# Gate arithmetic of a ConvFFN up-projection moved from SBUF scratch into PSUM banks, and a layer loop written out

## The chip, the cores and the metric

One core of one Trainium2 chip runs the program. The metric is device time in microseconds (us) of one execution. TensorE (PE) does the matmuls, VectorE (DVE) and ScalarE (ACT) the elementwise work, GpSimd (POOL) one subtraction per weight unit, and SyncE (SP) issues the weight loads.

## The reference

Two decoder layers run over 256 prompt tokens and 8 x 8 sample tokens, T = 320 columns in all. The part that the change touches is the second half of each layer, the ConvFFN:

```
h2 = rms_norm(x, p['norm2_g'])
a, b = jnp.split(h2 @ p['w_up'], 2, axis=-1)              # each (tokens, 2816)
a_seq = jnp.concatenate([conv_buf, a], axis=1)            # two earlier rows in front
c = p['conv_b'] + sum(a_seq[:, j:j + L] * conv_w[j] for j in range(3))
x = x + (jax.nn.gelu(c) * b) @ p['w_down']
new_buf = a_seq[:, a_seq.shape[1] - 2:]
```

## The kernel before

Weights come as units of 128 x 1024 floats, 148 per layer, in the order of use. Every matmul is made of three, so that it is nearly exact in float32: a unit is split into a rounded part `whi` and a rest `wlo`, activations into `hh`/`hl` or `oh`/`ol`, and the products whi x hi, whi x lo and wlo x hi add up in one PSUM bank. SP loads unit n into slot n % 4 of `raw` when that slot's last unit is split (L222). ACT makes `whi` (`hi`, L267), POOL makes `wlo` (`lo`, L231) into one of two slots, once PE is done with the unit two before. A unit is 24 matmuls of 128 x 128 by 128 x 320. All order between engines comes from counting semaphores; each engine works its program off in the order in which it is written.

The feature dimension of the ConvFFN is 22 tiles of 128 rows (FT). They are worked in two groups, 12 (FA) and 10 (FB): the up-projection of the group (`ups`), then its down-projection (`downs`). One tile is a pair of units: unit a into one PSUM bank, unit b into the next. Two pairs are in flight in four banks (A and C for the first group, B for the second); `s` is the pair's parity. Per layer that makes 24 + 12 + 20 + 10 = 66 units from the first up-unit to the last down-unit.

What follows for a pair, by line. DVE: L896 and L897 multiply bank a by the inverse rms `rs` into `apad` in SBUF, behind the two earlier rows that ACT puts there (L542). L901, L902 and L904 are the three taps of the convolution, SBUF to SBUF through three scratch tiles `cc`. ACT: L547 and L548 copy the convolution's new state out, L550 is the gelu into `gg`. DVE: L907 multiplies bank b by `rs` into `tb`, L909 and L910 multiply `gg` by `tb` into `ff`. ACT: L554 rounds `ff` into `oh`. DVE: L913 subtracts to get `ol`. ACT's two splits `hi(u + 4)` and `hi(u + 5)` of later units stand between these steps, the second behind the gelu. PE starts pair j when `ff` of pair j - 2 is there:

```
pe.wait_ge(f_ready, lv * FT + i * 2 + (j0 + s - 1 + 8))
up_unit(u0 + 2 * s, i, banks[2 * s], first)
up_unit(u0 + 2 * s + 1, i, banks[2 * s + 1])
```

The two layers are a hardware loop on each engine (`Fori`, L296 on ACT, L647 on DVE, L1022 on PE), and so are the pairs within `ups`; waits then take their values from registers. At the layer's end DVE adds the down-projection to `x` (L922), then at the next layer's start makes `hl` of the memory tokens (L652) and sums squares (L614), which PE reads in a matmul with ones (L1012).

Of the kernel before, what the change touches and what calls it, by code (L numbers as in the profile page):

```python
# [26 lines left out]
T = SEQ + NS  # L27
# [20 lines left out]
def build_trunk(nc, w, x_in, mem_in, cache_k, cache_v, st_in, consts, final_g,  # L48
# [6 lines left out]
    with ctx:  # L55
# [132 lines left out]
        ap_ready = sem("a_scaled")  # L188
        a_ready, c_ready, g_ready, f_ready, fh_ready, fl_ready = (sem(n) for n in ("conv_state_in_place", "conv_ready", "gelu_ready", "ff_ready", "ff_hi", "ff_lo"))
# [5 lines left out]
        carrier = sem("wait_carrier")  # L195
# [8 lines left out]
        def _(sp):  # L204
# [12 lines left out]
            with sp.Fori(1, DEPTH * UNITS // 4) as i:  # L217
                for s in range(4):
                    src = w[sp.snap(i * 4 + s)]
                    sp.wait_ge(hi_ready, i * 4 + s - 3)  # L220
                    sp.wait_ge(lo_ready, i * 4 + s - 3)
                    sp.dma_start(raw[:, s, :], src).then_inc(loaded[s], 16)  # L222


        @block.gpsimd
        def _(pool):
            def lo(u, s, l, iv=0):

                pool.wait_ge(hi_ready, l * UNITS + iv + u + 1)
                pool.wait_ge(unit_done, l * UNITS + iv + u - 1)  # L230
                pool.tensor_tensor(out=wlo[:, s % 2, :], in0=raw[:, s, :], in1=whi[:, s, :].bitcast(f32),  # L231
                                   op=ALU.subtract).then_inc(lo_ready, 1)

            with pool.Fori(0, DEPTH) as l:
# [3 lines left out]
                pool.wait_ge(hi_ready, l * UNITS + 2)  # L238
                pool.tensor_tensor(out=wlo[:, 1, :], in0=raw[:, 1, :], in1=whi[:, 1, :].bitcast(f32),
                                   op=ALU.subtract).then_inc(lo_ready, 1)  # L240
                lo(2, 2, l)
                lo(3, 3, l)
                with pool.Fori(1, UNITS // 4) as i:
                    for s in range(4):
                        lo(s, s, l, i * 4)
                pool.wait_ge(lo_ready, (l + 1) * UNITS)
# [3 lines left out]
        def _(act):  # L250
# [45 lines left out]
            with act.Fori(0, DEPTH) as lv:  # L296
                l[0] = lv
# [237 lines left out]
                def ups(u0, n, j0):  # L535
                    with act.Fori(0, n // 2) as i:
                        for s in range(2):
                            u = u0 + 2 * s
                            k = i * 2 + (s + j0)
                            sv = apad[s][:, 258:338].rearrange("p (b t) -> p b t", b=8)  # L540
                            act.wait_ge(f_ready, lv * FT + i * 2 + (j0 + s - 1 + 8))
                            nc.scalar.activation(sv[:, :, 0:2], par[:, bass.ds(k * 16 + C_CS, 16)].rearrange("p (b t) -> p b t", b=8),  # L542
                                                 ACT.Copy).then_inc(a_ready, 1)
                            done(u, i * 4)
                            hi(u + 4, i * 4)
# [5 lines left out]
                            done(u + 1, i * 4)  # L551
                            hi(u + 5, i * 4)
                            act.wait_ge(f_ready, lv * FT + i * 2 + (j0 + s + 1) + 8)
                            nc.scalar.activation(oh[:, i * 2 + s, :], ff[:, s, :], ACT.Copy).then_inc(fh_ready, 1)  # L554

                ups(U_UP1, FA, 0)
# [3 lines left out]
                ups(U_UP2, FB, FA)  # L560
                act.wait_ge(fh_ready, lv * FT + FT)
# [28 lines left out]
        def _(dve):  # L590
# [40 lines left out]
            dve.sem_inc(f_ready, 8)  # L631
# [15 lines left out]
            with dve.Fori(0, DEPTH) as lv:  # L647
                l[0] = lv
# [134 lines left out]
                for p in range(4):  # L783
# [25 lines left out]
                    dve.sem_inc(carrier, 1)  # L809
# [72 lines left out]
                def ups(j0, n, banks, u0):  # L882
                    base = dve_n[0]
                    dve.sem_inc(carrier, 1)
                    with dve.Fori(0, n // 2) as i:
                        def lk(ins, k):
# [56 lines left out]
        def _(pe):  # L943
# [78 lines left out]
            with pe.Fori(0, DEPTH) as lv:  # L1022
# [259 lines left out]
                def ups(u0, n, j0, banks, peel):  # L1282
# [6 lines left out]
                    with pe.Fori(1 if peel else 0, n // 2) as i:  # L1289
                        for s in range(2):  # L1290
                            up_pair(u0, j0, s, i, banks)
# [149 lines left out]
```

## Time and profile before

| | us |
|---|---|
| median of 3 runs | 1429.87 (1428.28 to 1432.77) |
| span of the profiled execution, first to last instruction | 1425.8 |
| median less that span | 4.07 |
| PE busy | 1301.5 (91%) |
| DVE busy | 837.2 (59%) |
| ACT busy | 582.5 (41%) |
| POOL busy | 714.2 (50%) |

Times below are from the start of that span. Matmuls are pipelined and their ends are modelled, so a matmul row's own duration (0.31 us) is longer than the distance to the next (0.15 us); the distance is what counts. Idle time of an engine costs something only where another waits for it.

### The profile page before, as it was taken

How to read it: one execution, taken by the hardware profiler on the slowest of the kernel's cores; microseconds unless marked ns; L12 is line 12 of the kernel's file. 1: busy time of each engine (PE TensorE's matmuls, PEld its weight loads, DVE VectorE, ACT ScalarE, POOL GpSimd, SP SyncE). 2: the span in 40 equal slices, each digit the busy share in tenths (PEclk: the TensorE clock that was granted, in tenths of full speed). 3: DMA queues.
4: the chain of work that ended last, by engine and by line, in shares of the span. 5: the costliest groups of instructions: out<-in, count | busy, mean ns of one | idle time of the engine just before them, and what ended most of it. 6: DMA issues, size and time to landing. Idle time of an engine off the chain costs nothing.

```text
span 1425.8 us, 24778 instructions
## 1 busy us (share of the span) xinstructions
PE 1301.5 (91%) x8240; PEld 1233.4 (87%) x8240; DVE 837.2 (59%) x1247; ACT 582.5 (41%) x951; POOL 714.2 (50%) x298
## 2 busy tenths in 40 slices
PE   3999998999999889988978999899999988899886
PEld 3799887999999879988968988899999988898885
DVE  4543328654776775378453541546749587726874
ACT  5472224433444544333444532324443545533342
POOL 2653324444666556655655343434446655566553
PEclk9999999999999999999989999999999999999998
DMA  7435333332444333433554444324334433344342
GB/s 288 148 120 191 133 106 128 117 115 91 149 147 135 116 117 128 152 120 117 178 176 142 148 148 144 111 90 135 124 115 148 141 126 104 117 148 148 103 145 74
DMA packets 53364, 191.90 MB, mean 135 GB/s; under 512 B 6048, under 2 KB 7328, under 8 KB 52896
## 3 DMA queue, kind: packets, MB, share of 16 engines
q1 hardware_dynamic: 43632, 159.15, 32.8%
q10 hardware_dynamic: 9648, 31.60, 6.2%
q8 instruction: 56, 0.92, 0.3%
q14 instruction: 28, 0.23, 0.0%
HBM read 182.20 MB, written 8.53 MB: 134 GB/s over the span
## 4 chain that ended last, share of the span: by engine, by line
PE 62%; DVE 21%; issue 7%; ACT 5%; POOL 2%; DMA 1%; DVEq 1%; ACTq 1%; SPq 0%; POOLq 0%
PE bank L989 27%; PE bank L958 18%; PE bank L1002 6%; DVE ol L913 5%; DVE arena L901 3%; DVE arena L902 3%; DVE arena L904 3%; ACT whi L267 2%; PE bank L1183 2%; POOL wlo L231 2%; DMA raw<-w 1%; PE bank L1086 1%; PE bank L1073 1%; DVE arena L896 1%; ACT oh L554 1%
## 5 line engine op out<-in xcount | busy, mean ns | idle before, releaser
L231 POOL TENSOR_TENSOR wlo<-raw,whi 128x1024 fp32r<-128x1024 f32 x292 | 709.3, 2430 | 668.7 <-PE bank L989 338.6
L267 ACT ACTIVATE whi<-raw 128x1024 fp32r<-128x1024 f32 x294 | 308.1, 1051 | 216.7 <-PE bank L958 91.3
L958 PE MATMUL bank<-hh,whi 128*128 128x320 f32 x832 | 266.7, 321 | 50.6 <-ACT whi L267 50.2
L989 PE MATMUL bank<-oh,whi 128*128 128x320 f32 x848 | 286.3, 338 | 19.6 <-DVE arena L754 8.9
L989 PE MATMUL bank<-ol,whi 128*128 128x320 f32 x848 | 283.5, 334 | 0.0
L989 PE MATMUL bank<-oh,wlo 128*128 128x320 f32 x848 | 282.8, 333 | 0.0
L958 PE MATMUL bank<-hl,whi 128*128 128x320 f32 x832 | 263.9, 317 | 0.0
L958 PE MATMUL bank<-hh,wlo 128*128 128x320 f32 x832 | 263.6, 317 | 0.0
L958 PEld LDWEIGHTS bank<-hh,whi 128*128 128x128 f32 x832 | 162.2, 195 | 58.6 <-ACT whi L267 56.9
L989 PEld LDWEIGHTS bank<-oh,whi 128*128 128x128 f32 x848 | 167.1, 197 | 27.4 <-issue 15.5
L989 PEld LDWEIGHTS bank<-oh,wlo 128*128 128x128 f32 x848 | 167.1, 197 | 3.4 <-issue 1.1
L989 PEld LDWEIGHTS bank<-ol,whi 128*128 128x128 f32 x848 | 167.2, 197 | 3.1 <-issue 0.2
L958 PEld LDWEIGHTS bank<-hh,wlo 128*128 128x128 f32 x832 | 162.3, 195 | 0.0
L958 PEld LDWEIGHTS bank<-hl,whi 128*128 128x128 f32 x832 | 162.0, 195 | 0.2
L958 PE MATMUL bank<-oh,whi 128*128 128x320 f32 x416 | 129.1, 310 | 7.3 <-POOL wlo L231 7.3
L958 PE MATMUL bank<-oh,wlo 128*128 128x320 f32 x416 | 128.5, 309 | 0.0
L958 PE MATMUL bank<-ol,whi 128*128 128x320 f32 x416 | 128.5, 309 | 0.0
L913 DVE TENSOR_TENSOR ol<-arena,oh 128x320 f32 x44 | 98.7, 2244 | 34.0 <-ACT oh L554 34.0
L477 ACT ACTIVATE arena<-bank,par 128x320 f32<-128x320 f32 x48 | 25.3, 528 | 150.1 <-PE bank L989 150.1
L958 PEld LDWEIGHTS bank<-oh,whi 128*128 128x128 f32 x416 | 78.1, 188 | 9.2 <-issue 6.9
L958 PEld LDWEIGHTS bank<-ol,whi 128*128 128x128 f32 x416 | 78.1, 188 | 0.0
L958 PEld LDWEIGHTS bank<-oh,wlo 128*128 128x128 f32 x416 | 78.1, 188 | 0.0
(192 smaller groups left out, 1875.3 us busy)
## 6 DMA issues: line engine op xcount, KB each, us to landing
raw<-w SPq DMA_DIRECT2D x296, 512.0 KB, 3.3
arena<-cache_k ACTq DMA_DIRECT2D x16, 512.0 KB, 5.2
arena<-cache_v ACTq DMA_DIRECT2D x16, 512.0 KB, 4.3
arena<-st_in ACTq DMA_DIRECT2D x8, 512.0 KB, 5.0
sst_out<-arena ACTq DMA_DIRECT2D x8, 512.0 KB, 2.7
arena<-mem_in ACTq DMA_DIRECT2D x2, 1024.0 KB, 6.2
con<-consts SPq DMA_DIRECT2D x1, 1288.0 KB, 13.1
x<-x_in SPq DMA_DIRECT2D x2, 640.0 KB, 9.2
```

Source lines behind the costliest of these rows:

```text
L231: pool.tensor_tensor(out=wlo[:, s % 2, :], in0=raw[:, s, :], in1=whi[:, s, :].bitcast(f32), op=ALU.subtract).then_inc(lo_ready, 1)
L267: nc.scalar.activation(whi[:, s, :], raw[:, s, :], ACT.Copy).then_inc(hi_ready, 1)
L477: nc.scalar.activation(G[:, j, :], A[u % 2][:, 0:T], ACT.Sigmoid, bias=par[:, C_BG + j:C_BG + j + 1]).then_inc(evac, 1)
L554: nc.scalar.activation(oh[:, i * 2 + s, :], ff[:, s, :], ACT.Copy).then_inc(fh_ready, 1)
L901: lk(V.tensor_scalar(cc[s][0][:, 0:336], apad[s][:, 0:336], cw(0), par[:, bass.ds(jw + C_CB, 1)], ALU.mult, ALU.add), 5 * s + 2)
L902: lk(V.scalar_tensor_tensor(out=cc[s][1][:, 0:336], in0=apad[s][:, 1:337], scalar=cw(1), in1=cc[s][0][:, 0:336], op0=ALU.mult, op1=ALU.add ...
L904: V.scalar_tensor_tensor(out=cc[s][2][:, 0:336], in0=apad[s][:, 2:338], scalar=cw(2), in1=cc[s][1][:, 0:336], op0=ALU.mult, op1=ALU.add).t ...
L913: V.tensor_tensor(out=ol[:, i * 2 + s, :], in0=ff[:, s, :], in1=oh[:, i * 2 + s, :].bitcast(f32), op=ALU.subtract).then_inc(fl_ready, 1)
L958: r = MM(out, a, b, start=first and i == 0, stop=last and i == 2, skip_group_check=True)
L989: r = MM(o, a, b[:, k, 0:n], start=k == 0 and i == 0, stop=k == KT_ - 1 and i == 2, skip_group_check=True)
L1002: r = MM(banks[a][:, :], x_[:, k, t0:t0 + P], w_, start=k == 0 and j == 0, stop=k == KT_ - 1 and j == 2, skip_group_check=True)
L1183: r = MM(B[2 + j // 2][:, (j % 2 * 2 + e) * P:(j % 2 * 2 + e + 1) * P], kTm[64:128, e, j * P:(j + 1) * P], vt[64:128, p // 2, 2, h * P:(h ...
```

## The change

The scratch tiles `cc`, `tb` and `ff` are dropped. ACT starts the convolution: it applies the first tap and the bias to `apad` and writes the result into bank a, whose matmul output has been read by then. DVE adds the other two taps in place in that bank. The gelu reads the bank. Bank b is multiplied by `rs` in place, then by `gg` in place, and both `oh` and `ol` are made from it. So each of the Vector instructions of a pair has one operand in PSUM. PE may start pair j only when `ol` of pair j - 2 is written (`fl_ready`), since the banks hold the data until then. The two state copies on ACT become one of 18 columns. All hardware loops, the layers' too, are written out, so waits take constants and no engine jumps back.

```diff
# ACT, per pair
-                            act.wait_ge(ap_ready, lv * FT + i * 2 + (j0 + s + 1))
-                            nc.scalar.activation(cout[:, k, 0:2], apad[s][:, 256:258], ACT.Copy)
-                            nc.scalar.activation(cout[:, k, 2:18].rearrange("p (b t) -> p b t", b=8), sv[:, :, 8:10], ACT.Copy)
-                            act.wait_ge(c_ready, lv * FT + i * 2 + (j0 + s + 1))
-                            nc.scalar.activation(gg[s][:, 0:336], cc[s][2][:, 0:336], ACT.Gelu_apprx_tanh).then_inc(g_ready, 1)
+                        act.wait_ge(ap_ready, 2 * (lv * FT + j + 1))
+                        act.wait_ge(a_ready, lv * FT + j + 1)
+                        nc.scalar.activation(ac[:, 0:336], apad[s][:, 0:336], ACT.Identity, scale=par[:, C_CW + j:C_CW + j + 1],
+                                             bias=par[:, C_CB + j:C_CB + j + 1]).then_inc(c0_ready, 1)
+
+                        nc.scalar.activation(cout[:, j, :].rearrange("p (b t) -> p b t", b=9),
+                                             apad[s][:, 248:338].rearrange("p (b t) -> p b t", b=9)[:, :, 8:10], ACT.Copy).then_inc(cv_ready, 1)
+                        act.wait_ge(c_ready, lv * FT + j + 1)
+                        nc.scalar.activation(gg[s][:, 0:336], ac[:, 0:336], ACT.Gelu_apprx_tanh).then_inc(g_ready, 1)
...
-                            nc.scalar.activation(oh[:, i * 2 + s, :], ff[:, s, :], ACT.Copy).then_inc(fh_ready, 1)
+                        nc.scalar.activation(oh[:, t, :], bc[:, 0:T], ACT.Copy).then_inc(fh_ready, 1)
# DVE, per pair
-                            lk(V.tensor_scalar(cc[s][0][:, 0:336], apad[s][:, 0:336], cw(0), par[:, bass.ds(jw + C_CB, 1)], ALU.mult, ALU.add), 5 * s + 2)
-                            lk(V.scalar_tensor_tensor(out=cc[s][1][:, 0:336], in0=apad[s][:, 1:337], scalar=cw(1), in1=cc[s][0][:, 0:336],
-                                                      op0=ALU.mult, op1=ALU.add), 5 * s + 3)
-                            V.scalar_tensor_tensor(out=cc[s][2][:, 0:336], in0=apad[s][:, 2:338], scalar=cw(2), in1=cc[s][1][:, 0:336],
-                                                   op0=ALU.mult, op1=ALU.add).then_inc(c_ready, 1)
-                            lk(V.tensor_tensor(out=tb[:, s, :], in0=bb[:, 0:T], in1=rs[:, :], op=ALU.mult), 5 * s + 4)
-                            lk(V.tensor_tensor(out=ff[:, s, 0:SEQ], in0=gg[s][:, 0:SEQ], in1=tb[:, s, 0:SEQ], op=ALU.mult), 5 * s + 5)
-                            V.tensor_tensor(out=ol[:, i * 2 + s, :], in0=ff[:, s, :], in1=oh[:, i * 2 + s, :].bitcast(f32),
-                                            op=ALU.subtract).then_inc(fl_ready, 1)
+                        dve.wait_ge(c0_ready, now)
+                        link(V.scalar_tensor_tensor(out=ac[:, 0:336], in0=apad[s][:, 1:337], scalar=cw(1), in1=ac[:, 0:336],
+                                                    op0=ALU.mult, op1=ALU.add))
+                        V.scalar_tensor_tensor(out=ac[:, 0:336], in0=apad[s][:, 2:338], scalar=cw(2), in1=ac[:, 0:336],
+                                               op0=ALU.mult, op1=ALU.add).then_inc(c_ready, 1)
+                        link(V.tensor_tensor(out=bc[:, 0:T], in0=bc[:, 0:T], in1=rs[:, :], op=ALU.mult))
+                        V.tensor_tensor(out=bc[:, 0:SEQ], in0=bc[:, 0:SEQ], in1=gg[s][:, 0:SEQ], op=ALU.mult).then_inc(f_ready, 1)
+                        V.tensor_tensor(out=ol[:, t, :], in0=bc[:, 0:T], in1=oh[:, t, :].bitcast(f32), op=ALU.subtract).then_inc(fl_ready, 1)
# PE, per pair
-                    pe.wait_ge(f_ready, lv * FT + i * 2 + (j0 + s - 1 + 8))
+                        if j >= 2:
+                            pe.wait_ge(fl_ready, lv * FT + j - 1)
# each engine
-            with pe.Fori(0, DEPTH) as lv:
+            for lv in range(DEPTH):
```

How the instructions stand, with the semaphores that they wait for, is shown at three places. First DVE in the up-projection, one pair (the first of a loop's two) of the kernel before; `arena` is the SBUF region that holds `apad`, `cc`, `gg`, `tb` and `ff`, `bank` a PSUM bank.

```order
L896 TENSOR_TENSOR arena<-bank,rs 128x256 [waits unit_done]
...
L897 TENSOR_TENSOR arena<-bank,rs 128x8x8 [waits vector_chain]
...
L901 ISA [waits conv_state_in_place,a_scaled]
L901 TENSOR_SCALAR arena<-arena,par 128x336
...
L902 SCALAR_TENSOR_TENSOR arena<-arena,par 128x336
...
L904 SCALAR_TENSOR_TENSOR arena<-arena,par 128x336
...
L907 TENSOR_TENSOR arena<-bank,rs 128x320 [waits unit_done]
...
L909 TENSOR_TENSOR arena<-arena 128x256 [waits gelu_ready,vector_chain]
...
L910 TENSOR_TENSOR arena<-arena 128x64 [waits vector_chain]
L913 ISA [waits ff_hi]
L913 TENSOR_TENSOR ol<-arena,oh 128x320
```

The same pair on DVE in the changed kernel, with its own line numbers:

```order
L884 TENSOR_TENSOR arena<-bank,rs 128x256 [waits unit_done]
L885 TENSOR_TENSOR arena<-bank,rs 128x8x8
L890 SCALAR_TENSOR_TENSOR bank<-arena,par,bank 128x336 [waits conv_started,a_scaled]
L892 SCALAR_TENSOR_TENSOR bank<-arena,par,bank 128x336 [waits vector_chain]
L895 TENSOR_TENSOR bank<-bank,rs 128x320 [waits unit_done]
L897 TENSOR_TENSOR bank<-bank,arena 128x256 [waits gelu_ready,vector_chain]
L898 TENSOR_TENSOR bank<-bank,arena 128x64
L902 TENSOR_TENSOR ol<-bank,oh 128x320 [waits ff_hi,ff_ready]
```

Nine data instructions became eight: the TENSOR_SCALAR is gone, a wait for ACT (`conv_started`) stands in its place, and every one of the eight names a bank.

Second, ACT in the same loop, one pair of the second group, before (L267 is the split into `whi`) and then in the changed kernel (L255 is):

```order
L542 ACTIVATE arena<-par 128x8x2
...
L267 ACTIVATE whi<-raw 128x1024 [waits unit_done,unit_loaded0]
...
L547 ACTIVATE cout<-arena 128x2
...
L548 ACTIVATE cout<-arena 128x16
L550 ACTIVATE arena<-arena 128x336 [waits conv_ready]
...
L267 ACTIVATE whi<-raw 128x1024 [waits unit_done,unit_loaded1]
...
L554 ISA [waits ff_ready]
L554 ACTIVATE oh<-arena 128x320
```

```order
L531 ACTIVATE arena<-par 128x8x2
L255 ACTIVATE whi<-raw 128x1024 [waits unit_done,unit_loaded0]
L537 ACTIVATE bank<-arena,par 128x336 [waits conv_state_in_place,a_scaled]
L540 ACTIVATE cout<-arena 128x18
L543 ACTIVATE arena<-bank 128x336 [waits conv_ready]
L255 ACTIVATE whi<-raw 128x1024 [waits unit_done,unit_loaded1]
L547 ACTIVATE oh<-bank 128x320 [waits ff_ready]
```

L537 is new and stands behind the first split; the second split still stands between the gelu (L543) and `oh` (L547). A load of ACT's function table stood twice in the first group's loop body before; written out, it stands once per layer, ahead of the first gelu.

Third, PE at the first matmul of a pair, before and then in the changed kernel:

```order
L1278 REGISTER_ALU
L948 REGISTER_ALU [waits ff_ready]
L958 MATMUL bank<-hh,whi 128x320 [waits lo_ready,hi_ready]
L958 MATMUL bank<-hl,whi 128x320
L958 MATMUL bank<-hh,wlo 128x320
```

```order
L944 MATMUL bank<-hl,whi 128x320
L944 MATMUL bank<-hh,wlo 128x320
L944 MATMUL bank<-hh,whi 128x320 [waits lo_ready,hi_ready,ff_lo]
L944 MATMUL bank<-hl,whi 128x320
L944 MATMUL bank<-hh,wlo 128x320
```

The wait for `ff` became one for `ol`, two steps later in the pair.

## Rows read from the trace of the kernel before

**Rows 1.** The page: span, and busy time of PE.

```profile
span 1425.8 us, 24778 instructions
PE 1301.5 (91%) x8240; PEld 1233.4 (87%) x8240; DVE 837.2 (59%) x1247; ACT 582.5 (41%) x951; POOL 714.2 (50%) x298
```

**Rows 2.** Stretches: window, length, busy (xcount) of PE, PEld, DVE, ACT, POOL; clock; DMA.

```profile
438.92:712.82 273.90, 245.16 (x1588) 240.12 (x1586) 179.91 (x219) 115.51 (x196) 158.55 (x65) 0.97 0.40 132
1136.04:1410.74 274.70, 245.34 (x1588) 240.13 (x1586) 180.34 (x219) 112.50 (x193) 158.63 (x65) 0.97 0.37 123
438.92:545.27 106.35, 91.84 (x580) 89.31 (x579) 82.58 (x100) 53.66 (x91) 58.58 (x24) 0.95 0.36 119
590.11:675.01 84.90, 74.92 (x482) 73.45 (x481) 67.39 (x80) 29.45 (x61) 48.83 (x20) 0.96 0.37 124
...
621.83:626.95 5.12, 5.12 (x24) 5.12 (x25) 4.00 (x6) 1.68 (x5) 2.33 (x1) 0.67 0.31 95
```

**Rows 3.** The chain that ended last, merged: start, length, what.

```profile
558.37 35.45 PE bank L958 x240
...
604.75 2.37 DVE arena L901
...
607.98 2.77 DVE arena L904
```

**Rows 4.** Waits, whole run: who waited for whom, total, times, longest.

```profile
PE bank L958 <- ACT whi L267: 50.2, 29, 2.3
...
PE bank L958 <- POOL wlo L231: 7.3, 7, 1.2
...
PE bank L1030 <- PEq L1025: 7.0, 1, 7.0
```

**Rows 5.** DVE, ACT and POOL in order of time, one up-projection pair.

```profile
616.01 0.23 DVE L897 TENSOR_TENSOR arena<-bank,rs 128x64 f32<-128x64 f32 x1
616.43 2.35 DVE L901 TENSOR_SCALAR arena<-arena,par 128x336 f32<-128x336 f32 x1 [0.20 <-DVE arena L897]
...
621.31 0.22 DVE L910 TENSOR_TENSOR arena<-arena 128x64 f32<-128x64 f32 x1
622.30 2.21 DVE L913 TENSOR_TENSOR ol<-arena,oh 128x320 f32 x1 [0.76 <-ACT oh L554]
...
620.66 1.04 ACT L267 ACTIVATE whi<-raw 128x1024 fp32r<-128x1024 f32 x1
621.66 0.47 ACT L554 ACTIVATE oh<-arena 128x320 f32 x1
...
616.19 2.40 POOL L231 TENSOR_TENSOR wlo<-raw,whi 128x1024 fp32r<-128x1024 f32 x1 [1.51 <-PE bank L958]
621.77 2.38 POOL L231 TENSOR_TENSOR wlo<-raw,whi 128x1024 fp32r<-128x1024 f32 x1 [3.18 <-ACT whi L267]
```

**Rows 6.** Single lines: count, shortest/median/longest in ns, first and last start.

```profile
L913 DVE TENSOR_TENSOR ol<-arena,oh x44: 2164/2220/2572, 455.8 to 1384.1; 128x320 f32 x44
...
L902 DVE SCALAR_TENSOR_TENSOR arena<-arena,par x44: 567/569/2487, 450.2 to 1380.7; 128x336 f32<-128x336 f32 x44
...
L907 DVE TENSOR_TENSOR arena<-bank,rs x44: 478/484/486, 453.6 to 1381.9; 128x320 f32<-128x320 f32 x44
...
L754 DVE SCALAR_TENSOR_TENSOR arena<-arena,par,bank x16: 535/548/549, 189.8 to 934.0; 128x320 f32<-128x320 f32 x16
...
L686 DVE TENSOR_TENSOR ol<-bank,oh x10: 424/424/425, 114.2 to 885.3; 128x256 fp32r<-128x256 f32 x10
...
L477 ACT ACTIVATE arena<-bank,par x48: 527/527/530, 240.2 to 1063.8; 128x320 f32<-128x320 f32 x48
...
L550 ACT ACTIVATE arena<-arena x44: 482/484/488, 453.7 to 1382.0; 128x336 f32<-128x336 f32 x44
```

**Rows 7.** DVE in order of time at the start of the second layer.

```profile
713.02 1.68 DVE L922 TENSOR_TENSOR x<-x,bank 128x320 f32<-128x320 f32 x4 [4.17 <-PE bank L958]
718.89 0.88 DVE L652 SCALAR_TENSOR_TENSOR hl<-arena,par,hh 128x256 fp32r<-128x256 f32 x2 [4.19 <-ACT whi L267]
```

More of the change, by code:

```diff
@@ L216, in _, with lo @@
             sp.dma_start(fg[:, :], final_g).then_inc(fg_s, 16)
[L217 to L222, printed above, removed]
+            for n in range(4, DEPTH * UNITS):
+                sp.wait_ge(hi_ready, n - 3)
+                sp.wait_ge(lo_ready, n - 3)
+                sp.dma_start(raw[:, n % 4, :], w[n]).then_inc(loaded[n % 4], 16)
         @block.gpsimd
         def _(pool):
[L227 to L231, printed above, removed]
+            def lo(u, l):
+                pool.wait_ge(hi_ready, l * UNITS + u + 1)
+                pool.wait_ge(unit_done, l * UNITS + u - 1)
+                pool.tensor_tensor(out=wlo[:, u % 2, :], in0=raw[:, u % 4, :], in1=whi[:, u % 4, :].bitcast(f32),
                                    op=ALU.subtract).then_inc(lo_ready, 1)
-            with pool.Fori(0, DEPTH) as l:
+            for l in range(DEPTH):
                 pool.wait_ge(hi_ready, l * UNITS + 1)
@@ L237, in _ @@
                 pool.wait_ge(last_done, l + 1)
[L238 to L245, printed above, removed]
+                for u in range(1, UNITS):
+                    lo(u, l)
                 pool.wait_ge(lo_ready, (l + 1) * UNITS)
@@ L556, in _, with ups @@
-                ups(U_UP1, FA, 0)
+                def ups(u0, n, j0, banks):
+                    for t in range(n):
+                        j, s, u = j0 + t, t % 2, u0 + 2 * t
+                        ac, bc = banks[2 * s], banks[2 * s + 1]
+                        if j >= 2:
+                            act.wait_ge(c_ready, lv * FT + j - 1)
+                        sv = apad[s][:, 258:338].rearrange("p (b t) -> p b t", b=8)
+                        k = C_CS + 16 * j
+                        nc.scalar.activation(sv[:, :, 0:2], par[:, k:k + 16].rearrange("p (b t) -> p b t", b=8),
+                                             ACT.Copy).then_inc(a_ready, 1)
+                        done(u)
+                        hi(u + 4)
+                        act.wait_ge(ap_ready, 2 * (lv * FT + j + 1))
[6 more added lines that the diff above has]
+                        nc.scalar.activation(gg[s][:, 0:336], ac[:, 0:336], ACT.Gelu_apprx_tanh).then_inc(g_ready, 1)
+                        done(u + 1)
+                        hi(u + 5)
+                        act.wait_ge(f_ready, 2 * (lv * FT + j + 1))
+                        nc.scalar.activation(oh[:, t, :], bc[:, 0:T], ACT.Copy).then_inc(fh_ready, 1)
@@ L645, in norm @@
                                         op=ALU.subtract).then_inc(hl_ready, 1)
-            with dve.Fori(0, DEPTH) as lv:
-                l[0] = lv
+            for lv in range(DEPTH):
+                l[0], dve_n[0] = lv, 0
                 dve.wait_ge(hi_ready, lv * UNITS + 1)
@@ L1020, in _ @@
             r.then_inc(rmt_done, 1)
-            with pe.Fori(0, DEPTH) as lv:
+            for lv in range(DEPTH):
                 l[0] = lv
@@ L1264, in _, with up_unit @@
                     unit(U_OUT + m, oh, ol, T, (mgl, lv * 8) if m == 0 else None)
-                def up_unit(u, i, bank, first=False):
-                    ready(u, i * 4)
+                def up_unit(u, bank, first=False):
+                    ready(u)
                     for k in range(KT_):
```

104 lines of the change are left out of this document (37 added, 67 removed).

## The prediction, made before the changed kernel had run

> **What bounds the kernel now.** I read the page first: PE is busy for 1301.5 of 1425.8 us, and no other engine for more than 59% [rows 1]. So time can only come from where PE pauses or runs slowly, and I looked for a stretch with a known amount of PE work. Where nothing disturbs PE, 240 matmuls take 35.45 us [rows 3]. A row lasts 0.31 us, so the distance from one to the next is (35.45 - 0.31) / 239 = 0.147 us. A unit of 24 takes 3.53 us and a pair 7.06.
>
> The change lies in the 66 units from the first up-unit to the last down-unit of a layer: 1584 matmuls, 232.9 us at that distance. The rows count 1588 there; for the four others I add 0.9 us, an estimate (three at 0.31). The two layers take 273.90 and 274.70 us [rows 2]. The excess is 40.1 + 40.9 = **81.0 us**. It is more than PE's idle time there (28.7 and 29.4 us), since PE also runs slower after a pause: one unit took 5.12 us at a mean granted clock of 0.67, so in part at the lower of its levels, 1.2 GHz in place of 2.4 [rows 2]. Most of it lies in the up-projections: 106.35 us for 12 pairs and 84.90 for 10, on average 191.25 / 22 = 8.69 us in place of 7.06. That is 22 x 1.63 = 35.8 us a layer; the remaining 4 to 5 stand behind them, in the first down-units.
>
> What does PE wait for there? The waits name ACT's `whi`, 50.2 us in 29 waits, and POOL's `wlo`, 7.3 [rows 4]. For `whi` that is not the true cause: the wait for `f_ready` stands right ahead, and in the pair shown `ff` is done at 621.31 + 0.22 = 621.53 (L910), and PE's next unit begins at 621.83 [rows 2, 5]. So PE waits for the arithmetic of the pair two before, and I asked why that is slow. L913 takes 2.2 us in all 44 cases, and its shortest is 2164 ns [rows 6]. It has 320 columns, as has L907, which takes 484 ns and has an operand in a bank. The timeline shows what L913 stands beside: it ends at 622.30 + 2.21 = 624.51, and POOL's `wlo` at 621.77 + 2.38 = 624.15. L901 runs 2.35 us, to 618.78, and POOL beside it to 618.59 [rows 5]. L902 takes 569 ns as a rule and 2487 at the longest. Operations with a bank operand show nothing of that: L907 478 to 486, L754 535 to 549, L686 424 to 425 [rows 6]. So a Vector instruction with all its tensors in SBUF is held while GpSimd runs, and one with a bank operand isn't. The chain names the same lines: L901 2.37, L904 2.77 us [rows 3].
>
> **The change, part by part.** *The operands in banks.* I add up a pair anew, from the end of unit a, with 0.13 to 0.2 us from one step to the next (L897 to L901, L910 to L554, L554 to L913) [rows 5]. Scaling bank a: 0.424 (as L686, 256 columns) + 0.23 (L897). First tap on ACT: 0.17 + 0.53 (L477, a bank operand and pointers). Two taps: 0.17 + 0.57, then 0.20 + 0.57 (L902 unheld; L754 says 0.548 at 320 columns). Gelu: 0.13 + 0.48 (L550). `gg` times bank b: 0.17 + 0.424 + 0.22 (L686, L910). `oh`: 0.13 + 0.47. `ol`: 0.17 + 0.48 (L907) [rows 5, 6]. The sum is **5.5 us**; `tb`, 0.48, runs on DVE beside the gelu. ACT's splits (1.04 each) can stand ahead of the first tap or of `oh`; where one is running they add up to about 0.5 us together, an estimate. In DVE's order one pair follows the other, so 5.5 to 6.0 us is the shortest period that this chain allows, below the 7.06 of PE. Then PE is the bound, the up-projection runs at its distance, and nearly all of 81.0 us goes.
>
> *The later release.* PE waits for `ol` in place of `ff`: 0.13 + 0.47 + 0.17 + 0.48 = 1.25 us later. What stands behind that wait is every matmul of the pair. But `tb` needs unit b, which ends 3.53 us after unit a; from there `ol` is ready after some 0.13 + 0.48 + 0.17 + 0.64 + 1.25 = 2.7 us, and PE is in the other pair for 7.06. It has 4.4 us to spare, so I cost this at nothing. Without that cover it would be 1.25 us in 40 pairs, 50 us.
>
> *The first tap on ACT.* DVE loses L901 and gains a wait for ACT; behind it stand the pair's other DVE instructions. It is in the 5.5. ACT's work in a pair is two splits 2.1, tap 0.53, copy and state some 0.4 (an estimate), gelu 0.48, `oh` 0.47: 4.0 of 7.06. POOL needs 2.4 us a unit of 3.53 [rows 5]. Both have room.
>
> *Writing a bank.* No row of before shows DVE or ACT writing into PSUM. The nearest rows read a bank: against SBUF operands at the same or near size they differ by 484 to about 0.47 to 0.57, so by hardly anything, and I take nothing more. For the upper bound I double the part that grows with columns. L907 against L686 gives (484 - 424) / 64 = 0.94 ns a column, so 0.32 us on an instruction of 336 columns and 0.24 at 256; over the tap, the two taps and `gg` times bank b that makes 1.3 us, and the period 6.8 to 7.3. That would cost at most 0.24 x 44 = 11 us. A gain below SBUF's times would change nothing, since PE is the bound.
>
> A rule of the Trainium skill speaks against this part: "VectorE: DVE Perf Modes", section "Rules for kernel authors", says for elementwise work on a matmul's output to accept the slow rate or to copy into SBUF first where many operations follow, and its table gives an instruction with a PSUM source 62 cycles more than one in SBUF, at 0.96 GHz some 65 ns. The rows of this case show no such addition at 320 columns. By the rule six instructions would lengthen the period by 0.4 us, an estimate from that page, to 5.9 to 6.4; PE would still be the bound and the sum the same.
>
> *The loops written out.* At the layer's end DVE stands still for 4.19 us between L922 and L652 [rows 7], and PE's own sequencer makes the first matmul L1030 wait 7.0 us, once [rows 4]. L922 ends at 714.70; L652 could follow at once, and PE with its result, so about 4.2 us sooner. PE is then paced by DVE's eight `hl`, so I take 3.5, between nothing and 7.0. In the pair loops the registers' work is hidden behind the waits; where nothing waits it is part of PE's distance in rows 3, which has loop bodies in it. Nothing more.
>
> **The sum.** The profiled span 1425.8 - 81.0 - 3.5 = 1341.3. The median of the runs is 4.07 above the span, which I add: **1345 us**. Its own range: 5 us above for pauses left at the groups' starts, 11 for the writes, 7 below for the boundary and the estimates: 1338 to 1356.
>
> **The rivals.** *Writes to PSUM are dear.* Suppose each of the six instructions that write a bank costs x more. Then the period is about 5.5 + 6x and binds from x = 0.26. At 0.38 it is 7.8, and 44 x 0.7 = 31 us come back, less some 4 for the first pairs of the four groups: 1372. For it: no row shows such a write. Against it: reading is as fast as SBUF. Chance 0.12.
>
> *The serial chain becomes slower than the stalls.* The same mechanism ends above 1430 when the period passes 8.69, from x = 0.53, which is each of these instructions twice as long as now. At x = 0.7 it is 9.7, 44 x 1.0 = 44 us slower: 1474. Only a bank's write that doubles an instruction could do it. Chance 0.03.
>
> *The operands don't free DVE.* If GpSimd holds a DVE instruction that has one SBUF operand and writes a bank, the hold only moves. L913 loses 2.21 - 0.48 = 1.73 us to it, L901 2.35 - 0.57 = 1.78. With the one of the two the period is 7.25 to 7.5, with both 9.0; in between, at 8.2, 44 x 1.14 = 50 us come back: 1395. Against it stand L754 and L686, which read a bank and one or two SBUF operands and never vary by more than 14 ns. Chance 0.06.
>
> *The banks are held too long.* PE finds its bank not free where `ol` comes later than 4.4 us after its latest need; I worked out that it comes 4.4 before it. Should ACT's order (a split that waits for a weight load, with the tap behind it) make each pair 1 us late at PE, 40 us come back: 1385. The rows show no such load wait in the pair of rows 5. Chance 0.03.
>
> The Trainium skill, "PSUM — Partial Sum Buffer", section "Summary: rules for kernel authors", says to empty banks promptly since PSUM is tight; this change does the opposite, and by that rule the last rival is the likely one. The rows speak against it, with four banks and 4.4 us to spare.
>
> **How the numbers follow.** My forecast has 0.73, the four rivals 0.12, 0.03, 0.06 and 0.03, and 0.03 is left for more than I forecast (below 1338). The range 1336 to 1372 holds the forecast and the nearer part of the first rival, some 0.8. Faster by over 0.3% (4.3 us, about what a measurement here can tell from no change) are the forecast and all but the second rival, and a piece of the third, whose period may be the old one: 0.95. Within 0.3%: 0.02. Slower: 0.03.
>
> **What the profile after would show.** `ol` (L902 there) at 0.48 us in place of 2.22, its longest near its median; no DVE instruction of the pair that lasts as long as POOL's; pairs 7.06 us apart, and each layer's region near 234 us; PE's waits for `whi` near nothing, no stretch of the up-projection at a lowered clock; DVE's busy time lower by 150 to 190 us (1.73 at L913 44 times, 1.78 at L901 in part of them, and L901 itself); L1030 waiting some 3 us. Wrong would be: a DVE or ACT instruction that writes a bank and lasts far above 0.57 us (first two rivals), one that ends with POOL's (third), or PE waiting for `ol` (fourth).

## The result, and the profile after

The changed kernel takes **1342.90 us** (median of 4 runs, 1339.77 to 1344.83), the kernel before 1431.32 beside it (median of 4). The ratio is 0.9365, 95% interval 0.9329 to 0.9402: faster by 6.4%. The forecast was 1345.

The page of the changed kernel first, the lines that answer to [rows 1]:

```profile
span 1342.1 us, 20963 instructions
PE 1280.7 (95%) x8240; PEld 1219.1 (91%) x8240; DVE 651.4 (49%) x1203; ACT 569.3 (42%) x926; POOL 710.4 (53%) x298
```

Then the stretches of [rows 2], with the columns of that group: the two layers' 66 units, and the two up-projections of the first layer.

```profile
439.00:672.55 233.55, 233.16 (x1588) 232.60 (x1586) 86.81 (x197) 112.78 (x192) 157.12 (x65) 1.00 0.47 160
1093.61:1327.11 233.50, 233.12 (x1588) 232.60 (x1586) 86.63 (x197) 107.59 (x182) 156.50 (x65) 1.00 0.43 146
439.00:524.64 85.64, 85.25 (x580) 84.86 (x579) 41.63 (x98) 48.03 (x88) 58.01 (x24) 1.00 0.44 148
566.88:637.28 70.40, 70.40 (x482) 70.40 (x481) 32.71 (x80) 36.82 (x69) 48.35 (x20) 1.00 0.45 150
```

PE is busy throughout, at a granted clock of 1.00. The ten pairs of the second group take 70.40 us, 7.04 each, where they took 84.90 [rows 2]. Of the 83.7 us by which the span fell, the two regions hold 40.35 + 41.20 = 81.6, and the way from the first region's end to the second's start 423.22 - 421.06 = 2.2.

One pair of the second group in order of time, as in [rows 5]: DVE, then POOL.

```profile
591.72 0.43 DVE L884 TENSOR_TENSOR arena<-bank,rs 128x256 f32<-128x256 f32 x1 [1.36 <-PE bank L944]
592.07 0.21 DVE L885 TENSOR_TENSOR arena<-bank,rs 128x64 f32<-128x64 f32 x1
593.49 0.57 DVE L890 SCALAR_TENSOR_TENSOR bank<-arena,par,bank 128x336 f32<-128x336 f32 x1 [1.21 <-ACT bank L537]
594.10 0.57 DVE L892 SCALAR_TENSOR_TENSOR bank<-arena,par,bank 128x336 f32<-128x336 f32 x1
595.24 0.50 DVE L895 TENSOR_TENSOR bank<-bank,rs 128x320 f32<-128x320 f32 x1 [0.57 <-PE bank L944]
595.78 0.43 DVE L897 TENSOR_TENSOR bank<-bank,arena 128x256 f32<-128x256 f32 x1
...
596.92 0.49 DVE L902 TENSOR_TENSOR ol<-bank,oh 128x320 fp32r<-128x320 f32 x1 [0.57 <-ACT oh L547]
598.76 0.42 DVE L884 TENSOR_TENSOR arena<-bank,rs 128x256 f32<-128x256 f32 x1 [1.35 <-PE bank L944]
...
591.83 2.42 POOL L225 TENSOR_TENSOR wlo<-raw,whi 128x1024 fp32r<-128x1024 f32 x1 [1.10 <-PE bank L944]
595.35 2.42 POOL L225 TENSOR_TENSOR wlo<-raw,whi 128x1024 fp32r<-128x1024 f32 x1 [1.10 <-PE bank L944]
```

The direction of waiting has turned: DVE now waits for PE, 1.36 us for unit a and 0.57 for unit b, and everything that DVE does for the pair is done in about 5.7 us, these 0.57 included. L895 to L902 run while POOL's `wlo` runs and last as long as ever. The single lines show it for all 44 pairs (shortest, median, longest in ns), beside [rows 6]:

```profile
L890 DVE SCALAR_TENSOR_TENSOR bank<-arena,par,bank x44: 571/573/576, 447.8 to 1290.3; 128x336 f32<-128x336 f32 x44
L895 DVE TENSOR_TENSOR bank<-bank,rs x44: 490/500/500, 448.9 to 1292.1; 128x320 f32<-128x320 f32 x44
L902 DVE TENSOR_TENSOR ol<-bank,oh x44: 491/491/493, 451.0 to 1293.8; 128x320 fp32r<-128x320 f32 x44
L537 ACT ACTIVATE bank<-arena,par x44: 616/618/636, 447.0 to 1289.6; 128x336 f32<-128x336 f32 x44
```

PE's waits no longer name the up-projection at all; the longest ones left are those of other stages, for sums of squares (L608):

```profile
PE bank L998 <- DVE arena L608: 24.1, 6, 12.1
PE bank L975 <- DVE arena L747: 8.5, 2, 4.3
...
PE bank L1016 <- PEq L1011: 0.5, 1, 0.5
```

So far the lines agree with the forecast, but for the last: PE's sequencer (PEq) holds up the second layer's first matmul for 0.5 us, where some 3 were forecast. They don't tell which part of the change did it, and that is what the runs were for.

### The profile page after: what moved, and what is told of

It reads as the page before. It is cut to its first block, busy times and chain, and to the rows that moved or that the text cites. A ratio compares the mean times of both kernels' runs of the same rounds, so it can differ in the third digit from the quotient of the medians.

```text
span 1342.1 us, 20963 instructions
## 1 busy us (share of the span) xinstructions
PE 1280.7 (95%) x8240; PEld 1219.1 (91%) x8240; DVE 651.4 (49%) x1203; ACT 569.3 (42%) x926; POOL 710.4 (53%) x298
## 3 DMA queue, kind: packets, MB, share of 16 engines
q1 hardware_dynamic: 43632, 159.15, 34.9%
## 4 chain that ended last, share of the span: by engine, by line
PE 88%; DVE 8%; ACT 2%; issue 1%; DMA 1%; POOL 0%; DVEq 0%; SPq 0%; ACTq 0%; POOLq 0%
PE bank L944 40%; PE bank L975 30%; PE bank L988 6%; PE bank L1169 2%; DVE arena L633 1%; PE bank L1059 1%; PE bank L1072 1%; DVE arena L608 1%; PE bank L1158 1%; DVE hl L645 1%; DVE arena L815 1%; PE bank L1188 1%; DVE arena L829 1%; PE bank L1192 1%; PE bank L1181 1%
## 5 line engine op out<-in xcount | busy, mean ns | idle before, releaser
L255 ACT ACTIVATE whi<-raw 128x1024 fp32r<-128x1024 f32 x294 | 310.4, 1056 | 319.5 <-PE bank L944 171.7
L944 PE MATMUL bank<-hh,whi 128*128 128x320 f32 x832 | 257.8, 310 | 0.1
L944 PE MATMUL bank<-hl,whi 128*128 128x320 f32 x832 | 257.1, 309 | 0.0
L944 PE MATMUL bank<-hh,wlo 128*128 128x320 f32 x832 | 257.1, 309 | 0.0
L944 PEld LDWEIGHTS bank<-hh,whi 128*128 128x128 f32 x832 | 156.2, 188 | 0.8 <-DVE hl L839 0.7
L944 PEld LDWEIGHTS bank<-hl,whi 128*128 128x128 f32 x832 | 156.2, 188 | 0.2
L944 PEld LDWEIGHTS bank<-hh,wlo 128*128 128x128 f32 x832 | 156.2, 188 | 0.0
L908 DVE TENSOR_TENSOR x<-x,bank 128x320 f32<-128x320 f32 x32 | 13.4, 482 | 115.7 <-PE bank L944 115.7
```

What stands on the lines that cost most here:

```text
L255: nc.scalar.activation(whi[:, s, :], raw[:, s, :], ACT.Copy).then_inc(hi_ready, 1)
L944: r = MM(out, a, b, start=first and i == 0, stop=last and i == 2, skip_group_check=True)
```

## Experiments: which part does it

Three things were changed at once: the loops, the engine of the first tap, and the place of the operands. The theory was that GpSimd holds a Vector instruction whose tensors are all in SBUF, that this hold is the excess, and that only banks as operands lift it. Its rivals gave the gain to the loops or to the tap's move. All ratios are against the kernel before, run beside. The diffs are shortened: arguments that stay as they are, and bookkeeping, are left out. Gate tensors are here `cc`, `tb` and `ff`; `gg` stays in SBUF in every kernel, and the scaling by `rs` always reads a bank.

**Only the loops written out** (tap on VectorE, `cc`, `tb`, `ff` in SBUF), from the changed kernel:

```diff
-  nc.scalar.activation(ac[:, 0:336], apad[s][:, 0:336], ACT.Identity, ...)
+  link(V.tensor_scalar(cc[s][0][:, 0:336], apad[s][:, 0:336], cw(0), ...))
-  V.scalar_tensor_tensor(out=ac, in0=apad, scalar=cw(1), in1=ac)
+  V.scalar_tensor_tensor(out=cc[s][1], in0=apad, scalar=cw(1), in1=cc[s][0])
-  V.tensor_tensor(out=ol[:, t, :], in0=bc[:, 0:T], in1=oh[:, t, :])
+  V.tensor_tensor(out=ol[:, t, :], in0=ff[:, s, :], in1=oh[:, t, :])
-  pe.wait_ge(fl_ready, lv * FT + j - 1)
+  pe.wait_ge(f_ready, 2 * (lv * FT + j - 1))
```

> The changed kernel with all gate tensors back in SBUF (first tap on VectorE, cc, tb and ff scratch, PE waiting for ff): of the change only the written-out loops remain. Theory (GpSimd holds a Vector instruction that has all its tensors in SBUF, and banks as operands lift that): ol stays at 2.2 us in all 44 pairs, the pairs stay 8.3 to 8.9 us apart, each layer's region stays at 265 to 274 us, only the boundary between the layers gains 2 to 4 us; 1415 to 1430 us. Rival (register waits and jumps of the loops cause the excess): pairs at 7.04 us, regions of 234 us, 1343 to 1350 us.

Measured: 1397.88 us, 0.976 (0.9712 to 0.9808). Between the two, and a miss for the theory: `ol` keeps its hold (median 2369 ns, held in 40 of 44 pairs), yet the first region falls to 258.38 us. With waits that take constants the profile names the true releaser: PE waits 34.9 us for `ff` (L899).

This kernel lacks more than the loops. The written-out code also dropped DVE's waits for its own results behind L896, L909 and L913 of the kernel before, merged the two state copies, and loads ACT's function table once per layer. One such wait can be seen in the rows: L897 begins 0.46 us after L896 in the kernel before (615.55 and 616.01), 0.35 after it in the changed one (591.72 and 592.07). The table loads are not the cause: with the loops kept they stand in the first group alone, and with the tap moved the pairs are 8.93 us apart in both groups. What the registers and jumps cost and what DVE's waits cost was not tried apart; "the loops" stands for all of it below.

**Banks and the tap on ScalarE, loops kept**, from the kernel before (waits keep their register values):

```diff
-  lk(V.tensor_scalar(cc[s][0], apad[s], cw(0), ...))
+  nc.scalar.activation(ac, apad[s], ACT.Identity, scale=par[:, bass.ds(k + C_CW, 1)], ...)
-  lk(V.scalar_tensor_tensor(out=cc[s][1], in0=apad[s], scalar=cw(1), in1=cc[s][0]))
+  lk(V.scalar_tensor_tensor(out=aa, in0=apad[s], scalar=cw(1), in1=aa))
```

> The kernel before, its hardware loops kept, with the banks as operands and the first tap on ScalarE. Theory of the hold: pairs at 7.04 us, regions of 234 us, and only the boundary (2 to 4 us) is lost against the changed kernel: 1343 to 1349 us. Rival of the loops: regions of 265 to 274 us, 1420 to 1430 us.

Measured: 1349.27 us, 0.941 (0.9364 to 0.9457), the first region 233.67 us. As the theory expected, at the upper edge of its range: with banks the loops cost nothing in the regions, only some us elsewhere. From the first region's end to the second's start it takes 424.26 us, 3.2 more than the changed kernel.

**Tap on ScalarE into SBUF, loops written out, no banks**: the first of these kernels with the ScalarE instruction kept, writing `cc[s][0]`.

> The first of these kernels with the first tap moved to ScalarE, but into SBUF: the division of work of the changed kernel without its operands in banks. Theory of the hold: the hold of the first tap goes, that of ol (2.2 us in all 44) and of part of the taps and products stays; pairs 7.7 to 8.5 us apart, 1370 to 1410 us. Rival (VectorE's chain was too long by the tap that moved to ScalarE): pairs at 7.04 us, 1343 to 1350 us.

Measured: 1341.94 us, 0.9362 (0.9313 to 0.9411). The rival's number, and as fast as the changed kernel without one gate tensor in a bank. The holds haven't gone: the second tap's median is 1362 ns and that of `gg` times `tb` 1937. DVE has no idle time left between two pairs, and the first region is 233.49 us all the same.

**The same move of the tap with the loops kept**, from the kernel before:

```diff
-  lk(V.tensor_scalar(cc[s][0], apad[s], cw(0), ...))
+  nc.scalar.activation(cc[s][0], apad[s], ACT.Identity, scale=par[:, bass.ds(k + C_CW, 1)], ...)
```

> The kernel before with the first tap moved to ScalarE and nothing else: loops kept, all gate tensors in SBUF. Theory (a pair's chain on VectorE, its holds included, must fit into PE's 7.04 us a pair; moving the tap takes 1.1 us or more from it, the loops' register waits put 0.5 to 0.6 on it): pairs 7.4 to 7.7 us apart, regions of 243 to 252 us, 1365 to 1390 us. Rival (moving the tap is enough by itself): pairs at 7.04 us, regions of 234 us, 1345 to 1352 us.

Measured: 1412.03 us, 0.985 (0.9816 to 0.9884), the first region 264.96 us. Slower than either expected: the two parts are worth 36 us (loops) and 19 us (tap) alone, and 92 together. Parts that don't add up point to a threshold.

**GpSimd's subtraction cut to 64 of 1024 columns**, from the kernel with only the loops written out:

```diff
-  pool.tensor_tensor(out=wlo[:, u % 2, :], in0=raw[:, u % 4, :], in1=whi[:, u % 4, :], op=ALU.subtract)
+  pool.tensor_tensor(out=wlo[:, u % 2, 0:64], in0=raw[:, u % 4, 0:64], in1=whi[:, u % 4, 0:64], op=ALU.subtract)
```

> The first of these kernels, all gate tensors in SBUF, with GpSimd subtracting 64 of a unit's 1024 columns (the rest of wlo is zeroed once, so the third product of most columns is left out; PE's instructions stay). Theory of the hold: no Vector instruction of the pair lasts over 0.7 us, ol about 0.5, pairs at 7.04 us, regions of 233 to 236 us; the time at or below that of the changed kernel, 1310 to 1345 us, since other stages lose their holds too. Rival (a bank operand is quicker in itself, or the chain in SBUF is too long without any hold): pairs above 7.5 us and regions above 244.

Measured: 1302.68 us, 0.9105 (0.9053 to 0.9157), below the theory's range by 7; the first region is 232.87 us.

```profile
L906 DVE TENSOR_TENSOR ol<-arena,oh x44: 491/492/494, 429.0 to 1248.9; 128x320 fp32r<-128x320 f32 x44
```

With every gate tensor in SBUF and the tap on VectorE, a GpSimd instruction of 0.32 us in place of 2.4 brings PE to its pace. So the hold is real, and it is the excess that is left without the loops (PE's own waits for `wlo`, 5.1 us in the kernel with only the loops written out, go with it). The time is also some 40 us below the changed kernel's, outside the regions. In the changed kernel 97 Vector instructions last over 0.15 us longer than the shortest of the same line and shape, 130 us in all; with the short subtraction none does. PE waits for `wlo` only 1.0 us in the changed kernel. So holds in the other stages are the likely reason; no run changed their operands.

## Experiments: the threshold

What did the fast kernel without banks do? Its `ol` and POOL's `wlo` in order of time:

```profile
594.49 0.49 DVE L904 TENSOR_TENSOR ol<-arena,oh 128x320 fp32r<-128x320 f32 x1 [0.61 <-ACT oh L549]
594.90 0.42 DVE L886 TENSOR_TENSOR arena<-bank,rs 128x256 f32<-128x256 f32 x1
...
594.57 2.68 POOL L227 TENSOR_TENSOR wlo<-raw,whi 128x1024 fp32r<-128x1024 f32 x1 [1.11 <-PE bank L946]
```

`ol` begins 0.08 us ahead of `wlo`, and it is `wlo` that is held (2.68 in place of 2.4). In the other kernels with the gate tensors in SBUF and the whole subtraction `ol` begins behind it as a rule: by 0.39 us with only the loops written out, by some 0.53 with the loops kept. The kernel with only the loops written out shows both orders within one run: in four of its pairs `ol` comes 0.08 us ahead and lasts 0.49 us, in two 0.08 behind and lasts 2.68 or 2.69. One of each:

```profile
601.27 0.49 DVE L903 TENSOR_TENSOR ol<-arena,oh 128x320 fp32r<-128x320 f32 x1 [0.61 <-ACT oh L547]
601.34 2.69 POOL L227 TENSOR_TENSOR wlo<-raw,whi 128x1024 fp32r<-128x1024 f32 x1 [1.10 <-PE bank L945]
...
590.86 2.69 DVE L903 TENSOR_TENSOR ol<-arena,oh 128x320 fp32r<-128x320 f32 x1 [0.61 <-ACT oh L547]
590.78 2.42 POOL L227 TENSOR_TENSOR wlo<-raw,whi 128x1024 fp32r<-128x1024 f32 x1 [0.95 <-PE bank L945]
```

So the order of the two starts decides whether `ol` pays 0.49 us or over 2, and each step that a pair loses or saves on its way can turn it. The loops cost such steps. Among them are register instructions of DVE's own sequencer (DVEq), 44 of each, right ahead of the second tap and of `ol` in the kernel with the tap moved and the loops kept; no line of this kind stands there with the loops written out:

```profile
L905 DVEq FUSED_REGOPS  x44: 57/60/77, 449.1 to 1363.6; - x44
...
L916 DVEq FUSED_REGOPS  x44: 82/84/86, 455.2 to 1367.1; - x44
L916 DVE TENSOR_TENSOR ol<-arena,oh x44: 2199/2229/2610, 455.3 to 1367.3; 128x320 f32 x44
```

**One more Vector instruction ahead of `ol`**, in the fast kernel without banks:

```diff
+  V.tensor_tensor(out=scratch, in0=bc[:, 0:T], in1=rs[:, :], op=ALU.mult)
   V.tensor_tensor(out=ol[:, t, :], in0=ff[:, s, :], in1=oh[:, t, :], op=ALU.subtract)
-  pe.wait_ge(f_ready, 2 * (lv * FT + j - 1))
+  pe.wait_ge(fl_ready, lv * FT + j - 1)
```

> The written-out kernel with the tap on ScalarE and all gate tensors in SBUF, which ran as fast as the changed one, with one more Vector instruction ahead of ol (bank b times rs into unused scratch, 0.41 to 0.49 us); PE waits for ol, as in the changed kernel, to keep the bank for it. In that kernel ol began 0.08 us ahead of GpSimd's next wlo in 43 of 44 pairs and lasted 0.49 us. Theory (it ran at PE's pace only because ol just came ahead of GpSimd; with banks the place in time doesn't matter): ol now begins behind wlo's start and lasts 2.0 to 2.6 us in most pairs, pairs 7.8 to 8.3 us apart, 1365 to 1400 us. Rival (the chain has the same room as the changed kernel's): 1339 to 1348 us, as with five such instructions there.

Measured: 1405.97 us, 0.981 (0.9771 to 0.9849): 64 us for 0.41 us of work in a pair.

```profile
604.07 0.49 DVE L904 TENSOR_TENSOR arena<-bank,rs 128x320 f32<-128x320 f32 x1 [0.61 <-ACT oh L549]
604.48 2.37 DVE L905 TENSOR_TENSOR ol<-arena,oh 128x320 fp32r<-128x320 f32 x1
...
604.15 2.35 POOL L227 TENSOR_TENSOR wlo<-raw,whi 128x1024 fp32r<-128x1024 f32 x1 [1.10 <-PE bank L947]
```

`ol` now comes 0.33 us behind `wlo` and ends 0.35 behind its end. Held in 31 of 44 pairs, it takes the time to 6 us above the range; the first region is 265.91 us at a mean granted clock of 0.96, with PE waits of up to 3.2 us for `ol`. The later wait for `ol` is part of this kernel too and was not tried alone there. DVE itself waits for PE only 8.1 us, in 7 of the 44 pairs, so its own chain with the holds sets the pace, and not PE's later start.

**Five and nine more instructions in the changed kernel**, the same line repeated ahead of its `ol`.

> The changed kernel with five more Vector instructions in each pair (bank b times rs into unused scratch, 0.49 us each, their results not used), ahead of ol: 2.4 us more in the chain. VectorE waits 1.36 us for unit a and 0.57 for unit b in a pair, so the period grows by 2.4 - 1.93 = 0.5 us, to 7.5. Theory with the banks' spare time (ol may come 4.4 us late before PE waits, and 12 pairs collect 5.6): 1343 to 1350 us. Rival (each pair's excess is paid, as the prediction's rivals were priced): 44 x 0.5 = 20 us, 1358 to 1366.

> The same with nine more instructions, 4.3 us: the period grows by 2.4 us, to 9.4. Theory with the spare time: (12 x 2.4 - 4.4 + 10 x 2.4 - 4.4) x 2 = 88 us, 1425 to 1440 us, PE waiting for ol in most pairs. Rival without spare time: 105 us, 1445 to 1455. Where nothing is bound by this chain: 1342.

Measured: with five 1343.12 us, 0.9371 (0.9335 to 0.9407), the first region 233.48: no cost. With nine 1387.06 us, 0.9676 (0.9638 to 0.9715), outside all that was expected, the first region 254.46, and now PE waits for `ol`:

```profile
L904 DVE TENSOR_TENSOR ol<-bank,oh x44: 481/481/483, 457.1 to 1342.3; 128x320 fp32r<-128x320 f32 x44
...
PE bank L946 <- DVE ol L904: 32.8, 32, 1.1
```

DVE's period, from one `ol` to the next, is 8.35 us with nine. I had counted 0.49 us for each; one follows the other after 0.40 to 0.41, 3.6 us for nine, so the chain without them needs 8.35 - 3.6 = 4.8 us in place of the 5.5 forecast. With five it needs 6.8, still under 7.04: that run shows the room in the chain and says nothing of the spare time at PE. The run with nine does: per layer (12 + 10) x (8.35 - 7.04) = 28.8 us of excess became 254.46 - 233.55 = 20.9, so 7.9 were covered, some 4 for each of the two groups where 4.4 were forecast.

In most pairs of that kernel `ol` begins 0.36 us behind `wlo`, about as late as where it is held (0.33 to 0.53), and it lasts 0.48 us in all 44. With a bank as one input the order of the two no longer counts.

## Experiments: which operand counts, and GpSimd in pieces

**First tap back on VectorE, from SBUF into bank a** (`V.tensor_scalar(ac, apad[s], ...)` for the ScalarE instruction, the other gate tensors in banks), and **first tap from ScalarE into SBUF, the second tap reading it and writing the bank**:

```diff
-  nc.scalar.activation(ac, apad[s], ACT.Identity, ...)
+  nc.scalar.activation(cc[s][0], apad[s], ACT.Identity, ...)
-  V.scalar_tensor_tensor(out=ac, in0=apad[s], scalar=cw(1), in1=ac)
+  V.scalar_tensor_tensor(out=ac, in0=apad[s], scalar=cw(1), in1=cc[s][0])
```

> The changed kernel with the first tap on VectorE again, read from SBUF and written into bank a. Theory (a bank among an instruction's operands, the output too, keeps GpSimd from holding it): the tap lasts 0.45 to 0.52 us in all 44 pairs, and PE stays at 7.04 us a pair: 1339 to 1346 us. Rival (only the inputs count): the tap lasts about 2 us wherever GpSimd runs, and the pair has less room, 1340 to 1360 us.

> The changed kernel with the first tap written by ScalarE into SBUF scratch; the second tap reads two SBUF operands and writes bank a. Theory (a bank as output is enough): it lasts 0.57 us in all 44 pairs. Rival (two inputs in SBUF are held, wherever the output goes): 1.3 to 2.6 us in most. The time is 1338 to 1348 us by either, since one hold fits into the room that a pair has.

Measured: 1344.92 us, 0.938 (0.9342 to 0.9418), and 1339.87 (one run). The line of the tap in the first, that of the second tap in the other:

```profile
L888 DVE TENSOR_SCALAR bank<-arena,par x44: 629/630/633, 450.2 to 1289.7; 128x336 f32<-128x336 f32 x44
```

```profile
L892 DVE SCALAR_TENSOR_TENSOR bank<-arena,par x44: 576/1096/2817, 446.4 to 1286.5; 128x336 f32<-128x336 f32 x44
```

A bank as output keeps the one-input instruction free (never held, though it lasts 630 ns where 454 was its unheld time into SBUF in the kernel with only the loops written out). It doesn't help the one with two inputs in SBUF, which lasts over 0.86 us in 43 of 44 pairs, though over 1.3 in only 16: the theory as worded is wrong there, and the rival holds. What counts for a two-input instruction is that one input is in a bank. The changed kernel has that in each of its eight.

The Trainium skill, "SBUF — State Buffer", section "Who interferes with whom", says that a Vector instruction with two SBUF inputs contends with a GpSimd one that reads SBUF, that one with at most one SBUF input contends only in the modes that use both ports, and that whichever issues first keeps the port. The trace agrees as far as it goes: the second tap with two SBUF inputs was held, the first tap with one SBUF input and its output in a bank never was, and 0.08 us of order decided. The engine's modes show in no row.

**GpSimd's subtraction of a unit in two, and in four instructions**, in the changed kernel:

```diff
-  pool.tensor_tensor(out=wlo[:, u % 2, :], ...).then_inc(lo_ready, 1)
+  for q in range(4):                                   # or 2
+      c = slice(q * UW // 4, (q + 1) * UW // 4)
+      r = pool.tensor_tensor(out=wlo[:, u % 2, c], in0=raw[:, u % 4, c], in1=whi[:, u % 4, c], op=ALU.subtract)
+  r.then_inc(lo_ready, 1)
```

> The changed kernel with GpSimd's subtraction of a unit in two instructions of 512 columns, about 1.3 us each in place of 2.41. Theory (a held Vector instruction waits for the end of the GpSimd instruction that runs): the holds in the other stages (2.4 to 2.7 us at the longest) fall to 1.2 to 1.8, and up to half of the 40 us that the kernel with the short subtraction was below comes in: 1320 to 1338 us. Rival (it waits until GpSimd has nothing to do, or GpSimd's own longer work, 2.6 us a unit, costs as much): 1341 to 1350 us.

> The same in four instructions of 256 columns, about 0.74 us each, 3.0 us a unit. Theory: holds of 0.6 to 1.2 us, 1310 to 1333 us, no slower than with halves unless GpSimd's 3.0 us of the 3.52 of a unit begin to make PE wait for wlo. Rival: 1341 to 1360 us.

Measured: halves 1347.67 us (1342.57 to 1349.84), 0.9404 (0.9363 to 0.9445); quarters **1334.20** us (1332.80 to 1338.89), 0.9322 (0.9283 to 0.9361). Holds do get shorter: the longest of another stage's `ol`, 2708 ns in the changed kernel (L860), is 1467 with halves and 1030 with quarters (L862 in both). With halves that bought nothing, in the rival's range, although DVE's busy time fell from 651.4 to 633.5 us. POOL works longer, 767.9 us in place of 710.4; but with quarters it works 874.5 and the time falls, so why halves bought nothing stays open. Quarters are the fastest of the complete kernels by median, just above the theory's range, and all of their four runs lie below all four of the changed kernel's; the intervals of the ratios overlap. If the difference holds, some 9 of the 40 us came back.

## Why the prediction was right, and where its reasons were not

**The regions.** The term of 81.0 us was 81.6. PE's distance as the floor, and that PE waited for `ff` though the profile named `whi`: both held. The short subtraction of GpSimd shows the hold as a cause, and the banks with the loops kept show that they lift the whole excess. The theory's wording was off: held are instructions with two inputs in SBUF, wherever the output goes, and the one-input tap from SBUF to SBUF; and `ol` is held only where `wlo` began first.

**The step that failed**, at no cost to the number, is the one on the loops: "the registers' work is hidden behind the waits" and "Nothing more". With banks it is so: the loops kept cost nothing in the regions. Without banks, written-out loops alone gave 36 us, 15.5 of them in the first region. Of these, 8.3 are PE's idle time (28.7 us before, 258.38 - 237.96 = 20.4 after), and 7.2 its busy time, part of it at a lowered clock (245.16 to 237.96): the granted clock of the region went from 0.97 to 1.00 with the shorter waits. The prediction looked at the loops' work where PE waits and at PE's distance, and not at the steps that they put into DVE's chain, which was the bound.

**What it didn't see** is that banks were not needed: it worked out that the new chain fits with banks, and not whether one with the holds would fit without. The forecast's number is reached by two ways: by banks, with the loops kept (0.941) or with the tap back on VectorE (0.938), and without banks by the loops and the tap together (0.9362). What banks buy is room: with them 2 us more in a pair cost nothing, without them 0.41 us, with the later wait for `ol`, cost 64. Why the kernel without banks settles at 7.04 us a pair, its holds included, is argued from two rows of its timeline and the run with one instruction more; where else the border lies was not measured.

**Sizes.** The chain was 4.8 us, forecast 5.5: the steps between DVE instructions take 0.04 us or less where one follows the other at once in the changed kernel (595.24 + 0.50 to 595.78), and I had read 0.13 to 0.20 from a kernel with loops. Writing a bank costs next to nothing in the change: 573 ns for a tap (569 into SBUF) and 500 for bank b times `rs` (484) [rows 6]; ScalarE's tap is quicker into the bank, 618 ns against 668 into SBUF. Only the one-input tap on VectorE, which the change doesn't have, took 176 ns more into a bank. The first rival and the slower one fall with that. The 65 ns more that the Trainium skill, "VectorE: DVE Perf Modes", section "The TRN2 errata — SBUF-src ops pay a fixed extra latency per instruction", gives for a PSUM source did not show here: `ol` takes 491 ns from a bank and, not held, 491 to 496 from SBUF. The third rival, a hold on an instruction with one SBUF operand that writes a bank, is wrong: L890 never lasts over 576 ns. A hold in spite of a bank as output does exist, of the instruction with two inputs in SBUF, which the change doesn't have. The fourth, banks held too long, falls by the run with five, which writes `ol` 2 us later at no cost.

**The later release** was free, as forecast: PE never waits for a pair's `ol` (L902) in the changed kernel, and the run with nine puts the spare time at some 4 us.

**The boundary** was forecast at 3.5 us. PE's first matmul comes 6.6 us sooner after the region's end, then waits for `hl`, `wlo` and the squares. Before, the first matmul and the first with the squares:

```profile
720.01 2.07 PE L1030 MATMUL bank<-hh,whi 128*128 128x256 f32 x8 [7.02 <-PEq L1025]
...
728.62 1.44 PE L1012 MATMUL bank<-arena,con 128*128 128x320 f32 x2 [3.50 <-DVE arena L614]
```

In the changed kernel:

```profile
673.10 1.19 PE L1016 MATMUL bank<-hh,whi 128*128 128x256 f32 x8 [0.45 <-PEq L1011]
675.25 1.22 PE L1019 MATMUL bank<-hh,wlo 128*128 128x256 f32 x8 [0.97 <-POOL wlo L225]
...
678.05 2.96 PE L1022 MATMUL bank<-hl,whi 128*128 128x256 f32 x7 [1.46 <-DVE hl L645]
684.57 0.90 PE L998 MATMUL bank<-arena,con 128*128 128x320 f32 x1 [3.57 <-DVE arena L608]
```

At that last matmul 728.62 - 684.57 - (712.82 - 672.55) = 3.8 us are left, and 2.2 at the next region's start (3.2 against the kernel with banks and loops); where the rest went, in the attention stages between, was not followed up. DVE's busy time fell by 185.8 us, forecast 150 to 190.

## What to carry to other kernels

When a Vector instruction's longest time is far above its median, look at what GpSimd does at that moment, and count its SBUF inputs: a second input moved into a bank takes it out of reach, a bank as output alone does not. Before crediting a change with such a lift, work out also whether the same chain would fit without it: where instructions are held until another engine's work ends, 0.1 us of order can decide over 2 us, and parts of a change that give 36 and 19 us alone can give 92 together. Room in a chain is worth measuring by itself, by idle instructions put into it.

## What the runs showed that was not expected

Register instructions right ahead of a Vector instruction took 57 to 86 ns each in the kernel with the tap moved and the loops kept, counted in no engine's busy time, 44 times each. PE's granted clock of a region was 0.96 and 0.97 where its waits reached 3.2 and 2.3 us, and 1.00 where the longest was 1.2 (loops written out alone) or 1.7 (tap moved alone). GpSimd's instruction was held by a Vector one that began 0.08 us earlier, 2.68 us in place of 2.4. The short subtraction shows some 40 us to be had outside the ConvFFN's regions, of which four pieces a unit gave back perhaps 9.
